# Seven-product phases of a decoder trunk: seams reordered, splits inside the last steps, two GpSimd waits

## What is computed

```python
def swiglu(x, w_gate_up, w_down):
    gate, up = jnp.split(x @ w_gate_up, 2, axis=-1)
    return (jax.nn.silu(gate) * up) @ w_down

for l in range(DEPTH):                      # DEPTH = 2
    h = h + 0.5 * swiglu(rmsnorm(h, ffn1_norm[l]), ffn1_w_gate_up[l], ffn1_w_down[l])
    u = rmsnorm(h, mix_norm[l])
    ...                                     # main and mem_out from the mixer
    h = h + jnp.concatenate([main, mem_out], axis=-1) @ w_out[l]
    h = h + 0.5 * swiglu(rmsnorm(h, ffn2_norm[l]), ffn2_w_gate_up[l], ffn2_w_down[l])
    if l == N_A_LAYERS - 1:
        shared_k, shared_v, shared_c = shared_fox_kv(h, kv_norm, kv_w, kv_b_f)
return rmsnorm(h, final_norm)
```

## Time and profile before

| | |
|---|---|
| median of 3 runs | 1988.91 us (1988.36 to 1989.27) |
| the profiled execution | 1988.13 us, span of its records 1986.4 us |
| TensorE busy | 1930.9 us |
| VectorE busy | 1387.8 us |
| ScalarE busy | 802.2 us |
| GpSimd busy | 524.5 us |

### The profile page before, as it was taken

The page is one execution under the profiler, slowest core; times in us unless marked ns, Lnnn a source line. Parts: engine busy times, 40 slices in busy tenths (PEclk is TensorE's granted clock), DMA queues, the critical chain, the costliest instruction groups (busy, mean ns, idle before and its releaser), DMA issues.

```text
span 1986.4 us, 31460 instructions
## 1 busy us (share of the span) xinstructions
PE 1930.9 (97%) x12113; PEld 1688.2 (85%) x12113; DVE 1387.8 (70%) x1499; ACT 802.2 (40%) x1076; POOL 524.5 (26%) x397
## 2 busy tenths in 40 slices
PE   9999999999999899999999999999999979999998
PEld 7888888888878799997888999997887769999787
DVE  6544333378966899998445899996447589999623
ACT  5422222255545444444233444444235444344423
POOL 1312220113713344441110344431011034444000
PEclk9999999999999999999999999999999999999999
DMA  6343323343311233333344333333350223333321
GB/s 193 103 124 103 94 73 102 111 149 101 100 58 43 64 85 106 102 88 102 87 116 151 85 106 99 91 107 88 94 209 22 64 64 85 105 105 89 123 96 64
DMA packets 313981, 196.27 MB, mean 99 GB/s; under 512 B 18543, under 2 KB 304896, under 8 KB 313394
## 3 DMA queue, kind: packets, MB, share of 16 engines
q1 hardware_dynamic: 309872, 182.29, 31.8%
q10 hardware_dynamic: 3138, 9.79, 1.4%
q0 software_dynamic: 896, 3.16, 0.4%
HBM read 188.75 MB, written 6.46 MB: 98 GB/s over the span
## 4 chain that ended last, share of the span: by engine, by line
PE 73%; DVE 14%; issue 6%; POOL 3%; ACT 2%; DMA 1%; DVEq 0%; SPq 0%; ACTq 0%; POOLq 0%
PE ps L680 23%; PE ps L682 22%; PE ps L681 22%; DVE w_lo L2298 6%; POOL tri L3265 2%; POOL tri_tmp L3263 1%; DVE hid_lo L2520 1%; DVE w_lo L2208 1%; DVE sums L2289 1%; PE ps L1442 1%; PE ps L1468 1%; DVE rstd L2223 1%; DVE w_lo L2304 0%; ACT w_hi L1533 0%; PE ps L1453 0%
## 5 line engine op out<-in xcount | busy, mean ns | idle before, releaser
L680 PE MATMUL ps<-x_hi,w_hi 128*128 128x256 f32 (+1 forms) x1790 | 601.7, 336 | 29.0 <-DVE w_lo L2298 25.4
L682 PE MATMUL ps<-x_hi,w_lo 128*128 128x256 f32 (+1 forms) x1790 | 586.4, 328 | 0.0
L681 PE MATMUL ps<-x_lo,w_hi 128*128 128x256 f32 (+1 forms) x1790 | 586.0, 327 | 0.0
L680 PEld LDWEIGHTS ps<-x_hi,w_hi 128*128 128x128 f32 x1790 | 341.1, 191 | 77.8 <-issue 34.3
L2208 DVE TENSOR_TENSOR w_lo<-raw,w_hi 128x2048 fp32r<-128x2048 f32 (+2 forms) x113 | 245.4, 2172 | 176.2 <-ACT w_hi L1533 176.2
L682 PEld LDWEIGHTS ps<-x_hi,w_lo 128*128 128x128 f32 x1790 | 341.4, 191 | 29.1
L681 PEld LDWEIGHTS ps<-x_lo,w_hi 128*128 128x128 f32 x1790 | 341.7, 191 | 26.5 <-issue 0.5
L1533 ACT ACTIVATE w_hi<-raw 128x2048 fp32r<-128x2048 f32 (+2 forms) x114 | 189.0, 1658 | 424.3 <-PE ps L682 423.4
L680 PE MATMUL ps<-t_x,w_hi 128*128 128x256 f32 x792 | 225.0, 284 | 2.9 <-DVE t_x L2270 2.9
L681 PE MATMUL ps<-t_x,w_hi 128*128 128x256 f32 x792 | 224.8, 284 | 0.0
L682 PE MATMUL ps<-t_x,w_lo 128*128 128x256 f32 x792 | 224.5, 283 | 0.0
(11 more groups left out here) (376 smaller groups left out, 3095.9 us busy)
## 6 DMA issues: line engine op xcount, KB each, us to landing
raw<-in_ffn_w_gate_up SPq DMA_DIRECT2D x174, 512.0 KB, 5.0
raw<-in_ffn_w_down SPq DMA_DIRECT2D x48, 384.0 KB, 3.9
raw<-in_ffn_w_down SPq DMA_DIRECT2D x48, 320.0 KB, 3.2
raw<-in_gdn_w_in SPq DMA_DIRECT2D x26, 512.0 KB, 4.8
raw<-in_ffn_w_down SPq DMA_DIRECT2D x20, 512.0 KB, 4.6
raw<-in_w_out SPq DMA_DIRECT2D x16, 512.0 KB, 4.5
raw<-in_kv_w SPq DMA_DIRECT2D x12, 512.0 KB, 4.4
raw<-in_mem_w_kv SPq DMA_DIRECT2D x8, 512.0 KB, 4.1
```

Of the source, the lines that this page charges most:

```text
L680: nc.tensor.matmul(dst, hi, xh, start=first, stop=False)
L681: nc.tensor.matmul(dst, hi, xl, start=False, stop=False)
L682: return nc.tensor.matmul(dst, lo, xh, start=False, stop=last)
```

## The change

It touches the three seven-product phases and what stands just ahead of and behind them.

- **Tile 0** (`seven_first`): all seven products of pairs 0 to 2 first, then all of pair 3; before, products 2, 1, 5, 4 of all four pairs, then 6, 3, 7. The signals of finished products follow, and the wait for `part_taken` goes.
- **Weights ahead of feeds** (wout0, wout1): round and cut of the projection's last unit stand ahead of the feeds of pair 1, before behind them; S2 and S4 of tile 0 behind the feeds of pair 1, the direct cut and the S1 cut of tile 0 ahead of the last step of pair 2 (t_lo); the S3 round and cut of tile 0 ahead of pair 3. GpSimd adds S1 of tile 0 after the second square, S1 of tile 1 after the sixth.
- **Tile 1's direct blocks** are rounded and cut in two pieces, three pairs and one, the first when tile 0's pairs 0 to 2 are through products 1 and 4. S2 and S4 of tile 1 stand between the pieces. In step 1 the reciprocal and gate_scale stand behind the direct cut of tile 2.
- **Splits inside**: tiles of `hid` are stored in another order (`tile_at`: tile n = 2, 3, 4 at places 19 to 21, tile n of 5 or more at n - 3), and tiles 0 to 4 are split in steps 16 to 20 (one each, between S4 and the direct cut). Four more follow before the first down unit is cut, two behind the partial sums of tile 21. The second down unit is cut right behind the last gate_scale, before behind five more splits.
- **Two GpSimd waits** in each step from 2 on: `product` waits for S2 and S4 (`dve_sum`), `third_sum` waits for the direct cut (`direct_lo`, in all steps).
- **Loads** of tiles 3 to 21 wait for the third sum of the tile two before (`pool_sum`), before for its last cut (`lo_ready`).

The core of the diff:

```diff
@@ the storage of gate*up tiles
+FREE_TILES = 5
...
+        def tile_at(idx, n):
+            if idx == 0 or n < T4_TILES:
+                return n
+            return n + 17 if n < FREE_TILES else n - 3
@@ SyncE
-            def load(u0, parts, i=0):
-                if u0 >= 2:
+            def load(u0, parts, i=0, summed=None):
+                if summed is not None:
+                    sp.wait_ge(pool_sum, summed + 4 * i)
+                elif u0 >= 2:
                     sp.wait_ge(lo_ready, u0 - 1 + 2 * i)
@@ TensorE, seven_first
+                for kk in range(last_pair):
                     pe.wait_ge(pair_ready, 2 * (PAIRS * x + kk) + 2)
+                    pe.wait_ge(t_ready, PAIRS * x + kk + 1)
+                    part(2, direct_at(u, 2), "B21", kk, first=True)
+                    part(1, direct_at(u, 0), "B11", kk, first=True)
                     if kk == 0:
                         pe.wait_ge(sums_lo, (NP + 1) * x + 1)
+                    part(5, early_sum, "T1", kk, first=True)
+                    done = part(4, direct_at(u, 1), "T4", kk)
+                done.then_inc(product_done, 1)
                 pe.wait_ge(sums_lo, (NP + 1) * x + 2)
...
                 pe.wait_ge(lo_ready, u + 1)
...
+                pe.wait_ge(pair_ready, 2 * (PAIRS * x + last_pair) + 2)
+                part(2, direct_at(u, 2), "B21", last_pair)
...
@@ ScalarE, up phases
+                        if n == 0:
+                            act.wait_ge(product_done, done + 1)
+                            direct_round(u, 1, slice(0, PAIRS - 1))
+                            act.wait_ge(product_done, done + 2)
+                            direct_round(u, 1, slice(PAIRS - 1, PAIRS))
@@ VectorE, wout0 and wout1
-                        feed_pair(name, n)
+                        if n == 3:
+                            seven_lead_last(u + 4)
                         if n == 1:
                             cut_lo(u + 3)
-                        if n == 2:
-                            seven_lead(feeds[name], u + 4)
-                        if n == 3:
-                            seven_lead_last(u + 4)
+                        feed_pair(name, n, (lambda: seven_lead(feeds[name], u + 4)) if n == 2 else None)
+                        if n == 1:
+                            second_sum(feeds[name], u + 4, 0)
@@ VectorE, up phases
+                        if n == 0:
+                            next_direct(0)
                         second_sum(name, u, n + 1, i)
-                        direct_cut(name, u, n + 1, i)
+                        if split is not None:
+                            split_lo(split)
...
+                    for n in range(FREE_TILES):
+                        step(tail + n, (tail + n) % 2, split=n)
@@ GpSimd, up phases
+                        if n or fed_by[name] == "kv0":
+                            first_sum(u, n + 1, sums_used + n + 2, i)
+                        if n > 1:
+                            after_second(n + 1, i)
                             product(n - 1, 1 - j, i)
+                        after_direct(n + 1, i)
                         third_sum(u, n + 1, i)
+                        if n == 1:
+                            product(0, 0)
```

266 lines of the change are left out of this document (146 added, 120 removed).

## The result

The changed kernel takes 1938.92 us (median of 4 runs, 1937.87 to 1939.83); the kernel before, on the same chip, 1989.09 us (4 runs, 1988.36 to 1989.64). The ratio is 0.9748, 95% interval 0.9731 to 0.9765. The profiled execution took 1937.87 us, its records span 1936.1 us; before 1988.13 and 1986.4. So 50.3 us are gone where the prediction had 55.2.

A forecast was written before the change was run, and what follows sets the result against it. VectorE, blocked by GpSimd, was taken to pace the steady tiles at 10.60 us. Terms 29.7 + 15.4 + 0.7 + 10.4 - 1.0 = 55.2 us off 1988.1 gave 1932.9, stated as 1933; forecast range 1923 to 1944, with rivals 1921 to 1953.

The forecast's parts named there:

- Steady tiles: Tiles 3 to 21 of up1 and up3, 1 to 21 of up2: period 10.60 to 10.07 us, 29.7 us less.
- the second case of the forecast: Steady tiles: product meets the direct cut each time, 1.28 us more, VectorE's chain 9.9 us, still below 10.07.
- Splits in steps: Last five steps of each phase: a split adds 0.6 us to VectorE; cost booked 0.3 a phase, -1 us.
- Heads of up1 and up3: Start of both phases: tile 1 comes 5.2 us earlier, tile 1 to 3 2.5 less; 15.4 us for both.
- the last feed 1.3 to 3.8 us sooner, take 2.2: Ahead of tile 1 in up1 and up3: earlier TensorE release, less delays and collisions, brings the last feed 2.2 us sooner.
- Rival B: Heads of up1 and up3 keep their length, giving 3 instead of 15 us: 1945 us; chance 0.13.
- Tile 1 to 3: Up1 and up3, reciprocal behind tile 2's direct cut: 23.7 us becomes 21.2, 2.5 us less a head.
- Head of up2: First tiles of up2: the split direct cut leaves about 0.3 of a 1.04 us wait, 0.7 us less.
- Tails: Down phases: 5.2 us of waits for low parts and down3's wait and low clock go; 10.4 us less.
- A: Steady tiles: VectorE still paces at 10.3 to 10.6 us through collisions of product and direct cut; 1948 to 1963; 0.20 with D.
- C: Steady tiles: the two waits close a ring over two engines, up to 12.2 us a tile, 2052 us; chance 0.04.
- D: Steady tiles: block moves from weight sums to direct cut, VectorE as long as before, 1963 us; chance 0.20 with A.

The follow-up runs named there:

- extra_cut: The changed kernel with one more VectorE subtraction of 1.13 us, which ran in every second tile (8 a phase); 1950.21 us.
- w_tail: The kernel before with the two GpSimd waits, the new storage order, the splits inside the steps and their tail order; heads and loads as before; 1945.32 us.
- no_waits: The changed kernel without both GpSimd waits, with the loads of before; 1986.50 us.
- w_only: The kernel before with the two GpSimd waits and nothing else; 1952.86 us.
- small_squares: The changed kernel with GpSimd's additions of squares cut to 16 of 512 columns for six of eight blocks, result not complete; 1926.29 us.

## Why the prediction held, and where it missed

The time (1933 us forecast, 1938.92 measured) is 5.9 us above the forecast and inside the range. The range is not what the prediction's own bounds give: with heads of 5 to 21 and tails of 6 to 10.5 its sum runs from 1928 to 1948.5 us, not from 1923 to 1944. The measured time lies in both. Term by term, from the table:

- **Steady tiles: 29.7 forecast, 29.0 measured** (9.2 and 9.25 in tiles 3 to 21, 10.5 in up2). The mechanism is the one forecast: the sums are no longer blocked, TensorE paces at 10.08. Two details were wrong. The product does not run in a gap of VectorE; it meets the direct cut in nearly every tile. The working put the end of the sums 1.35 us ahead of that cut, but with a block in the chain everything is about 1.1 us later and the gap shrinks to 0.33 us. That was the second case of the forecast (9.9 us a tile; 9.75 measured), so the sum did not change; but VectorE's room was 0.33 us in these rows and 0.5 in extra_cut, not 1.5. And two waits were taken to be needed where one is enough.
- **Splits in steps: -1.0 forecast.** The stretch from tile 17 to the first down product is 50.83 us, five tiles of 10.08 and 0.43 more in up1, 0.25 in up2, 0.16 in up3: it held (0.3 a phase). In w_tail, with the old heads, the same stretch is 50.40, 50.68 and 50.40. no_waits shows the price without cover, 0.6 us a step.
- **Heads of up1 and up3: 15.4 forecast, 10.2 measured** (up1 3.2 until tile 1 and 1.7 to tile 3; up3 6.2 less 2.6 for hid_lo in the same stretch, and 1.6). The waits alone gave 1.0 of it (w_only). This is the term that was mis-sized, and the step in it was "the last feed 1.3 to 3.8 us sooner, take 2.2", for which the prediction shows no sum. That feed began at 673.87 us before and at 673.92 after: nothing. In up3 it is 0.4 us sooner, counted from the down phase ahead and without hid_lo. The chain behind it was right (5.7 forecast, 674.88 to 680.30 = 5.4 measured). Collisions were in the forecast, without saying how many: in up1 four of VectorE's instructions ahead of the feed stood for GpSimd's squares, 4.2 us, and 4.4 us is what small_squares takes off the path to it. Against before, though, this is not all new. From the second unit on (641 to 674 us) VectorE's rows have 5.4 us of blocked time before (the plain cut of 2.29 us took 3.38, an x_lo of 0.75 took 1.79, S2 and S4 1.78 and 1.67) and 6.0 after. The S3 cut (0.93 us) now lies ahead of the feed as well. VectorE's idle on this path fell by 0.8 us (5.2 to 4.4), and the blocks and the S3 cut put it back. TensorE's earlier release brought nothing: in up3 the 5.8 us wait of the earlier trace rows is now a 5.4 us wait for the direct cut of tile 0, and tile 0 then starts at a low clock (below). VectorE's path, not TensorE's, sets tile 1. Rival B (the heads keep their length) described this; it was right for the half of the term ahead of the last feed.
- **Tile 1 to 3: 2.5 forecast a head, 1.7 measured.** Tile 1 takes 10.88 us in up1: the clock fell again (0.52 granted from 680 to 682 us), behind the wait for the squares, which no step of the prediction had; without it tile 1 takes 10.17 (small_squares). So the low clock cost about the 0.8 us that the prediction had for it. Tile 2 takes 11.14, in small_squares too, where the prediction had 0.3 us over the pace and 1.06 are measured: it put the chain behind the reciprocal 0.2 us late. TensorE stands for the first cut, which comes behind the reciprocal, and this matmul starts 0.74 us after the one before it, where they follow at 0.12; the restart and the last cut of the tile (699.25) cost the rest:

```profile
696.12 0.39 PE L692 MATMUL ps<-x_hi,w_hi 128*128 128x256 f32 x1 [0.47 <-DVE w_lo L2339]
```

- **Head of up2: 0.7 forecast, 1.6 measured** (4.2 us in the stretch from down1, 2.6 of them hid_lo). w_only has 1.2 of it: the waits help there too.
- **Tails: 10.4 forecast, 9.9 measured** (5.2 of hid_lo, 4.7 in down3 of 5.25). In down3 a wait of 0.6 us for the last gates is new.
- **Loads: 0 forecast, 0.4 us between the medians**, less than can be told apart.
- **Rivals A, C, D.** A named the collision of product and direct cut in every tile. It does occur, but ends at 9.75 us, not at 10.3. C, the ring over two engines, would have begun to cost at 11.15 us a tile (55.2 us spread over 56 periods of 10.07 give 11.06); the steady tiles of the changed kernel stay at 10.08. D is refuted by w_only.

Added up, with the 0.4 us that tile 21 takes longer in up1 and up2: 29.0 + 10.2 + 1.6 + 9.9 - 0.4 = 50.3 us, the difference of the spans.

The forecast treated the parts as a sum. They are not one: 36.3 us for the waits alone and 2.7 for the rest alone are 39 us, together they give 50.2. The difference is 11 us. By the table it lies mostly where VectorE has no room without the waits: tiles 3 to 21 of up1 and up3 and 1 to 21 of up2 take 9.2 us longer in no_waits than before, and tiles 1 to 3 take 4.1 longer.

Two rows on the low clock (busy us of PE, PEld, DVE, ACT, POOL; granted clock; DMA), the changed kernel at the head of up3, where TensorE had been idle for 5.4 us until 1574.74:

```profile
1570.00:1575.00 5.00, 0.26 (x1) 0.26 (x2) 3.74 (x6) 3.51 (x7) 0.51 (x1) 0.78 0.00 0
1575.00:1580.00 5.00, 4.96 (x24) 4.66 (x25) 5.00 (x4) 1.40 (x2) 2.76 (x3) 0.54 0.00 0
```

0.54 of 2.4 GHz is close to the lower of the two levels, 1.2 GHz, for nearly all of the 5 us behind the idle. Tile 1 of up3 shows no cost of it: the last feed to the start of tile 1 takes 5.4 us in up3 as in up1, and VectorE is busy for most of that.
